# Expert value rows of two prompt tiles: one dense pass over the table in place of row gathers

## The chip, the core and the metric

One Trainium2 chip; the kernel runs on one of its cores. The metric is the device time of one execution in microseconds, the median of several. All data are fp32.

## What is computed

One layer of a decoder for 512 prompt tokens and 64 sample tokens (8 sequences of 8), D = 2048. The layer is: an input projection, latent attention (8 heads; the sample tokens also over 2048 cached tokens each) beside gated linear attention (4 heads), an output projection and residual; then the expert layer, and last an embedding gated by a sigmoid. What the change touches is the expert layer, cut from the reference:

```python
q = (xb @ w["peer_w_q"]).reshape(PEER_BLOCK, PEER_HEADS, 2, PEER_DKEY // 2)   # 8 heads
s1 = jnp.einsum("thd,kd->thk", q[:, :, 0], w["peer_keys1"])                    # 128 keys
s2 = jnp.einsum("thd,kd->thk", q[:, :, 1], w["peer_keys2"])                    # 128 keys
v1, i1 = lax.top_k(s1, PEER_TOPK)                                              # 16
v2, i2 = lax.top_k(s2, PEER_TOPK)
cand = (v1[..., :, None] + v2[..., None, :]).reshape(...)
cidx = (i1[..., :, None] * PEER_N_KEYS + i2[..., None, :]).reshape(...)
top_s, sel = lax.top_k(cand, PEER_TOPK)
e = jnp.take_along_axis(cidx, sel, -1)
gate = jax.nn.softmax(top_s.astype(F32), -1)
act = jax.nn.gelu(jnp.einsum("td,thkd->thk", xb, w["peer_u"][e]).astype(F32), approximate=False)
coef = (gate * act).astype(xb.dtype)
return jnp.einsum("thk,thkd->td", coef, w["peer_v"][e])
```

So every token picks 8 x 16 = 128 of 16384 experts, i.e. of 128 x 128 pairs of keys. It needs their rows of peer_u (for a dot product) and of peer_v (for a weighted sum). Each table has 16384 rows of 8 KB, 134.2 MB.

## The kernel before

Tokens lie in five tiles: 0 to 3 are prompt tiles of 128 tokens, 4 is the 64 sample tokens. They pass the mixer in groups, GROUPS = [[0], [1, 2], [3, 4]]. For a group, `mixer_loads` (SyncE), `mixing` (TensorE), `mixer` (VectorE and ScalarE) make the input projection, latent attention (for tile 4 the sample attention over cached pages), linear attention, the output projection and the query projection. This is the chain, all in the SBUF tile `front`. Weights come in slabs of 128 x 2048 (1 MB) into four buffers `W`, loaded by SyncE, each freed by the semaphore `slabs_used`. The input projection of group 1 is made ahead, beside the mixer of tile 0.

The queries give key scores. `best_keys` (VectorE) finds the best 16 of 128 keys for each head and side, `route` combines them to 16 experts a head with their gates and writes `idx_all` and `gate_all`, one column a pick.

The expert rows are gathered. A unit is one head of one prompt tile, 16 columns; the sample tile's 8 heads are folded into 4 units by spreading its 64 tokens on 128 partitions. For each column GpSimd issues an indirect DMA (`gathers`, L2540) that brings 128 rows of 8 KB, one for each token, into one of the RING = 8 buffers `ring`. VectorE takes it: a row of peer_u by one multiply-and-reduce with the token's input into `dots` (`dot_products`, L1968), a row of peer_v by a multiply-and-add into `total` (`weighted_sum`, L1993). Between the two, ScalarE applies GELU to the 16 dots of a unit and `gated` multiplies them with the gates. The order of gathers is GATHERS: unit u's peer_u rows, then unit u-1's peer_v rows. There are 36 units, so 576 gathers of each table.

VectorE and ScalarE must do the chain's steps and the gathers' work in one program order each. Tables of numbers set it: ROWS_BEFORE says, for each step of VectorE's chain, how many gathers are taken before it; STEPS_BEFORE says, for each unit, how many steps of ScalarE's chain come before its GELU; PAGES_BEFORE places the gathers of cached pages among GpSimd's. VectorE's order is walked so:

```python
def row_taken():
    rows_taken[0] += 1
    while steps_taken[0] < len(ROWS_BEFORE) and ROWS_BEFORE[steps_taken[0]] <= rows_taken[0]:
        step()
```

A step whose input is not there holds all that stands behind it, the gathers too; a gather's buffer is free only when VectorE has taken it.

At the end of a tile its sum is added to h in `xrow` and stored to `h2_dram` (`store_h2`, GpSimd). The gated embedding follows in groups, PLE_GROUPS = [[0, 1], [2, 3], [4]] (`embedding_loads`, `embedding`): h2 rows are loaded back, normed, projected with w_ple_gate (16 slabs) and w_ple_proj (2 slabs), and the result is stored. The last group, tile 4, has no store of h2 in between; its projection by w_ple_gate begins when the last gather is summed (`sample_embedding`).

## Time and profile before

| | us |
|---|---|
| median of 3 runs | 4337.45 |
| lowest and highest run | 4336.12, 4348.39 |
| span of the profiled execution (first to last instruction) | 4331.6 |
| VectorE (DVE) busy in the span | 3288.1 |
| TensorE (PE) busy | 2254.9 |
| GpSimd (POOL) busy | 2201.2 |
| ScalarE (ACT) busy | 522.0 |

The profiled execution has no run time of its own beside its span of 4331.6 us; the median lies 5.9 us above that span. The span is cut into windows by stage, in which the busy time of each engine, the granted clock of TensorE (1.00 is 2.4 GHz, 0.50 is 1.2 GHz) and what the 16 DMA engines moved can be read. A DMA share of 1.0 is all 16 engines busy all the time. The multiply-and-reduce of a gather leaves two records on DVE, one fp32 matmul leaves two on PE.

### The profile page before, as it was taken

The numbers are of one execution on the slowest core, as the hardware profiler recorded it, in microseconds if no ns is written. First come the engines' busy times: TensorE is split into PE (matmuls) and PEld (weight loads), VectorE is DVE, ScalarE is ACT, GpSimd is POOL, SyncE is SP. The second block draws the span as 40 slices with busy tenths as digits, with TensorE's granted clock in tenths as the row PEclk, the third lists the DMA queues.
The fourth block names the chain that finished last, engine by engine and source line by source line (L and its number), as shares of the span: only waits on it lengthen the run. The fifth ranks groups of instructions, "written<-read, shape, count | busy, mean of one in ns | idle before, by whom it ended". The sixth has DMA issues, their size and how long they took to land.

```text
span 4331.6 us, 24058 instructions
## 1 busy us (share of the span) xinstructions
PE 2254.9 (52%) x8238; PEld 1342.1 (31%) x8238; DVE 3288.1 (76%) x3700; ACT 522.0 (12%) x1098; POOL 2201.2 (51%) x1216
## 2 busy tenths in 40 slices
PE   8999815425899492779942457710000920000755
PEld 4456403213475131367731222710000410000322
DVE  0130699997667998868889856699999699988673
ACT  2220112122002001212212010000001000001001
POOL 0000365744332556468775653345667368877441
PEclk9999956657999796767865678955555965555877
DMA  8658789988997999989999899988989999999996
GB/s 294 250 223 287 303 357 364 422 323 335 424 423 299 422 424 414 353 356 365 406 374 360 347 400 413 405 345 339 399 365 405 424 415 422 422 407 422 424 408 234
DMA packets 261153, 1599.51 MB, mean 369 GB/s; under 512 B 27763, under 2 KB 49459, under 8 KB 91750
## 3 DMA queue, kind: packets, MB, share of 16 engines
q0 software_dynamic: 176064, 1268.30, 72.0%
q1 hardware_dynamic: 83078, 320.64, 19.5%
q10 hardware_dynamic: 1888, 9.03, 0.5%
q8 instruction: 65, 1.06, 0.1%
q14 instruction: 58, 0.48, 0.0%
HBM read 1554.75 MB, written 42.56 MB: 369 GB/s over the span
## 4 chain that ended last, share of the span: by engine, by line
PE 31%; DVE 30%; POOL 16%; DMA 13%; issue 7%; ACT 2%; SPq 0%; DVEq 0%; ACTq 0%; POOLq 0%
POOL ring L2549 16%; PE bank L826 14%; DVE ring L1968 11%; DVE total L1993 9%; DMA ring<-in_peer_v,idx_all 5%; DMA ring<-in_peer_u,idx_all 5%; PE bank L1251 4%; PE bank L1288 3%; PE bank L929 1%; PE bank L891 1%; PE bank L800 1%; PE bank L1079 1%; DMA front<-in_cache_kv_latent,page_rows 1%; DVE front L1744 1%; PE bank L1093 1%
## 5 line engine op out<-in xcount | busy, mean ns | idle before, releaser
L1993 DVE SCALAR_TENSOR_TENSOR total<-ring,gate_all,total 128x2048 f32<-128x2048 f32 x571 | 1341.8, 2350 | 188.0 <-DMA ring<-in_peer_v,idx_all 164.5
L2549 POOL DMA_INDIRECT ring<-in_peer_u,idx_all x576 | 1062.2, 1844 | 795.7 <-DVE total L1993 359.1
L2549 POOL DMA_INDIRECT ring<-in_peer_v,idx_all x576 | 1072.2, 1861 | 711.9 <-DVE total L1993 376.3
L1968 DVE CUSTOM_DVE_ANT_0 ring<-ring,xrow 128x2048 f32<-128x2048 f32 x576 | 1297.5, 2287 | 169.4 <-DMA ring<-in_peer_u,idx_all 167.5
L826 PE MATMUL bank<-front 128*128 128x512 f32 (+3 forms) x1920 | 838.3, 594 | 68.9 <-ACT front L2115 64.6
L800 PE MATMUL bank<-inv_diag,front 128*128 128x128 f32 (+1 forms) x304 | 61.9, 391 | 1159.3 <-DVE inv_diag L1378 1102.2
L826 PEld LDWEIGHTS bank<-front 128*128 128x128 f32 (+1 forms) x1920 | 338.4, 181 | 558.5 <-issue 554.5
L800 PEld LDWEIGHTS bank<-inv_diag,front 128*128 128x128 f32 (+1 forms) x304 | 58.9, 299 | 1164.2 <-DVE inv_diag L1378 1098.2
L1251 PE MATMUL bank<-front 128*128 128x128 f32 (+2 forms) x1536 | 257.0, 329 | 20.5 <-DMA front<-in_peer_w_q 17.4
L1251 PEld LDWEIGHTS bank<-front 128*128 128x128 f32 x1536 | 239.8, 192 | 39.3 <-DMA front<-in_peer_w_q 20.3
L2574 POOL DMA_DIRECT2D ring<-in_w_in x12 | 10.7, 894 | 342.8 <-PE bank L1288 239.6
L1373 DVE RECIPROCAL st<-st 128x1 f32<-128x1 f32 (+1 forms) x20 | 3.2, 161 | 225.8 <-ACT st L2049 225.8
L1288 PE MATMUL bank<-ring 128*128 128x490 f32 x384 | 163.8, 574 | 2.1 <-ACT front L2115 2.1
L2485 ACT ACTIVATE dots<-dots 128x16 f32<-128x16 f32 x36 | 7.7, 215 | 804.2 <-DVE dots L1968 759.3
L913 PE MATMUL bank<-ident,front 128*128 128x128 f32 (+1 forms) x20 | 4.6, 380 | 170.9 <-DVE front L1426 99.4
L1288 PEld LDWEIGHTS bank<-ring 128*128 128x128 f32 x384 | 70.4, 190 | 74.7 <-issue 71.6
L1196 PE MATMUL bank<-front 128*128 128x128 f32 (+1 forms) x288 | 41.7, 314 | 93.0 <-DVE front L1695 81.9
L2501 POOL DMA_DIRECT2D xrow<-xn_dram x6 | 3.4, 573 | 163.1 <-DMA z_dram<-total 102.7
L1079 PE MATMUL bank<-ident,front 128*128 128x128 f32 x256 | 74.8, 395 | 7.4 <-DMA front<-in_cache_kv_latent,page_rows 5.8
L1575 DVE MAX8 front<-front 128x8 f32<-128x128 f32 (+1 forms) x80 | 19.2, 281 | 76.4 <-ACT front L2325 75.5
L1415 DVE TENSOR_TENSOR g_mla<-g_mla 128x128 f32<-128x128 f32 x1 | 0.3, 291 | 100.3 <-DMA g_mla<-in_qk_gain_q 100.3
L1119 PE MATMUL bank<-front 128*64 128x256 f32 x256 | 70.5, 444 | 6.9 <-ACT front L2357 6.9
(323 smaller groups left out, 2894.0 us busy)
## 6 DMA issues: line engine op xcount, KB each, us to landing
front<-in_w_in SPq DMA_DIRECT2D x64, 980.0 KB, 8.4
front<-in_w_out SPq DMA_DIRECT2D x48, 1024.0 KB, 9.1
front<-in_peer_w_q SPq DMA_DIRECT2D x48, 1024.0 KB, 13.3
front<-in_w_ple_gate SPq DMA_DIRECT2D x48, 1024.0 KB, 9.1
ring<-in_w_in POOLq DMA_DIRECT2D x12, 1960.0 KB, 10.5
front<-in_w_uq SPq DMA_DIRECT2D x6, 1536.0 KB, 10.7
ring<-in_peer_u,idx_all POOLq DMA_INDIRECT x576, 14.3
ring<-in_peer_v,idx_all POOLq DMA_INDIRECT x576, 16.0
```

Of the source, the lines that this page charges most:

```text
L800: mm = e.matmul(out, row, inv_diag[:R, :R], start=True, stop=True)
L826: mm = e.matmul(bank[4 * sl + c][:R, 0:ncol], XT[:, k, sl * P:sl * P + R], W[:, n % SLABS, c * ncol:(c + 1) * ncol], start=(k == 0), stop= ...
L891: mm = e.matmul(bank[c][:R, :], XT[:, k, 0:R], W[:, n % SLABS, c * BANK:(c + 1) * BANK], start=(k == 0), stop=False)
L929: mm = e.matmul(bank[j][:R, 0:2 * QK], cqT[:, slot(t), k, 0:R], wq[:, k, j * 2 * QK:(j + 1) * 2 * QK], start=(k == 0), stop=(k == 3))
L1079: e.transpose(bank[k][:, j * P:(j + 1) * P], latb[:, i, k * P:(k + 1) * P], ident[:, :])
L1093: mm = e.matmul(S, lt[0:ROPE, 2, j * P:(j + 1) * P], qrT[0:ROPE, b, :], start=False, stop=True)
L1119: e.matmul(bank[7][0:NS, 0:KVR], pTs[:, pg, :], latb[:, pg % HALF, :], start=(pg == 0), stop=False)
L1251: mm = e.matmul(bank[j][:, 0:ntok], W[:, n % SLABS, at:at + P], XT[:, k, 0:ntok], start=(k == 0), stop=(k == KD - 1))
L1288: mm = e.matmul(bank[6 + sl][:, 0:IN_BANK], xt[:, k, sl * P:(sl + 1) * P], chunk(n)[:, k % 8, :], start=(k == 0), stop=(k == KD - 1))
L1968: e.tensor_tensor_reduce(out=ring[:, b, :], in0=ring[:, b, :], in1=xrow[:, t % 2, :], scale=1.0, scalar=0.0, op0=ALU.mult, op1=ALU.add, ac ...
L1993: e.scalar_tensor_tensor(out=total, in0=ring[:, b, :], scalar=c1, in1=total, op0=ALU.mult, op1=ALU.add).then_inc(s("summed"), 1)
L2549: e.indirect_dma_start(out=ring[:, k % RING, :], out_offset=None, in_=a[("peer_u", "peer_v")[side]][0], in_offset=bass.IndirectOffsetOnAxi ...
```

## The change

The peer_v rows of tiles 1 and 2 are no longer gathered. Their weighted sums are one matrix product: for each token a row of 16384 coefficients, zero but for its 128 picks, times the whole of peer_v, read once in 128 slabs of 128 rows. All peer_u rows, and the peer_v rows of tiles 0, 3 and 4, are gathered as before. The work stands behind the last group's routing, in this order:

1. `spread` for tile 1, later for tile 2: VectorE splits the picked expert number into its two key numbers (shift by 7, and with 127). TensorE transposes both and the coefficients, so that the 128 picks of a token lie on partitions. For each token VectorE makes two one-hot matrices 128 picks x 128 keys, the first scaled by the coefficient, and TensorE multiplies them: 128 x 128 coefficients of that token. Four tokens make a group, written to one PSUM bank; ScalarE copies it, and after each 16 tokens stores 1 MB to `c_dram`.
2. `expert_sums`: SyncE loads the 128 slabs of peer_v, and for every 8 slabs the coefficients of 256 tokens (`coefficients`, runs of 512 bytes); ScalarE turns them (`turned_coefficients`), and TensorE makes 8 matmuls of 128 x 512 a slab into all eight PSUM banks.
3. VectorE adds the banks to h of tiles 1 and 2, which are then the first embedding group: PLE_GROUPS = [[1, 2], [0, 3], [4]].

The gathers are now in tiles' order: both tables for tile 0, peer_u alone for tiles 1 and 2, both for tiles 3 and 4. The three tables of numbers are new. Some semaphores are merged, and the constant `iota16` (16 numbers) becomes `iota` (128).

```diff
+DENSE, SUMMED = [1, 2], [0, 3, 4]
+EB = 8
+GROUP = 4
+CHUNK = 16
+G_GROUPS = P // GROUP
+G_CHUNKS = P * len(DENSE) // CHUNK
...
 GATHERS = []
-for _u in range(UNITS):
-    GATHERS.append((_u, 0))
-    if _u:
-        GATHERS.append((_u - 1, 1))
-GATHERS.append((UNITS - 1, 1))
+for _t in range(T):
+    for _u in range(FIRST_UNITS[_t], FIRST_UNITS[_t + 1]):
+        GATHERS.append((_u, 0))
+        if _t in SUMMED and _u > FIRST_UNITS[_t]:
+            GATHERS.append((_u - 1, 1))
+    if _t in SUMMED:
+        GATHERS.append((FIRST_UNITS[_t + 1] - 1, 1))
...
@@ SyncE
+            def expert_rows(lo, hi):
+
+                for i in range(lo, hi):
+                    n = PASSES["dense"] + i
+                    e.wait_ge(s("slabs_used"), n - SLABS + 1)
+                    if n % SLABS in (PICKS_SLAB, ONEHOT_SLAB) and i < SLABS:
+                        e.wait_ge(s("g_psum"), G_GROUPS * len(DENSE))
+                    e.dma_start(W[:, n % SLABS, :], a["peer_v"][0][i * P:(i + 1) * P, :]).then_inc(s(f"w_landed{n % SLABS}"), 16)
+
+            def coefficients(b):
+
+                if b == 0:
+                    for i in range(2):
+                        e.wait_ge(s(f"c_stored{i}"), 16 * G_CHUNKS // 2)
+                if b >= 2:
+                    e.wait_ge(s("coefs_turned"), 2 * (b - 1))
+                e.dma_start(CB[b % 2].rearrange("p c i n -> p c (i n)"), c_dram[:, :, EB * b:EB * (b + 1), :].rearrange("c p i n -> p c (i n)"))\
+                    .then_inc(s(f"pair_landed{b % 2}"), 16)
...
@@ TensorE
+            def spread(j):
...
+                for q in range(G_GROUPS):
+                    n = j * G_GROUPS + q
+                    e.wait_ge(s("picks_spread"), n + j + 2)
+                    if n >= 2:
+                        e.wait_ge(s("g_staged"), n - 1)
+                    for i in range(GROUP):
+                        mm = e.matmul(bank[4 + n % 2][:, i * P:(i + 1) * P], onehot[:, n % 2, 1, i, :], onehot[:, n % 2, 0, i, :],
+                                      start=True, stop=True)
+                    mm.then_inc(s("g_psum"), 1)
+
+            def expert_sums():
+
+                e.wait_ge(s("g_staged"), G_GROUPS * len(DENSE))
+                for i in range(NKEY):
+                    n = PASSES["dense"] + i
+                    e.wait_ge(s(f"w_landed{n % SLABS}"), slab_landed(n))
+                    if i % (EB // 2) == 0:
+                        e.wait_ge(s("coefs_turned"), i // (EB // 2) + 1)
+                    for sl in range(len(DENSE)):
+                        cols = CT[:, i % EB, sl * P // CHUNK:(sl + 1) * P // CHUNK, :].rearrange("p c n -> p (c n)")
+                        for c in range(4):
+                            mm = e.matmul(bank[4 * sl + c][:, :], cols, W[:, n % SLABS, c * BANK:(c + 1) * BANK],
+                                          start=(i == 0), stop=(i == NKEY - 1))
+                    mm.then_inc(s("slabs_used"), 1)
...
@@ VectorE
+            def spread(j):
...
+                e.wait_ge(s("gates_ready"), j + 1)
+                if j == 0:
+                    e.wait_ge(s("slabs_used"), PASSES["dense"])
...
+                for q in range(G_GROUPS):
...
+                    for i in range(GROUP):
+                        k = GROUP * q + i
+                        e.tensor_scalar(onehot[:, n % 2, 0, i, :], iota[:, :], picksT[:, j, 0, k:k + 1], picksT[:, j, 2, k:k + 1],
+                                        ALU.is_equal, ALU.mult)
+                        ins = e.tensor_scalar(onehot[:, n % 2, 1, i, :], iota[:, :], picksT[:, j, 1, k:k + 1], None, ALU.is_equal)
+                    ins.then_inc(s("picks_spread"), 1)
...
                     dot_products(u, t)
-                    if u:
-                        weighted_sum(u - 1)
-            weighted_sum(UNITS - 1)
+                    if u > FIRST_UNITS[t]:
+                        if t in SUMMED:
+                            weighted_sum(u - 1)
+                        else:
+                            gated(u - 1)
...
@@ ScalarE
+            def turned_coefficients():
+
+                half = EB // 2
+                for m in range(NKEY // half):
+                    b, i = m // 2, m % 2 * half
+                    yield
+                    e.wait_ge(s(f"pair_landed{b % 2}"), 16 * (H_GLA // 2 + b // 2 + 1))
+                    if b:
+                        e.wait_ge(s("slabs_used"), PASSES["dense"] + EB * (b - 1) + i + half)
+                    e.copy(CT[:, i:i + half, :, :], CB[b % 2][:, :, i:i + half, :].rearrange("p c i n -> p i c n")).then_inc(s("coefs_turned"), 1)
```

How the instructions move is set by the tables of numbers. In the whole of VectorE's order the change has 576 gathers of peer_u and 320 of peer_v. At the chain's marks these many gathers have been taken, before and now: norm ahead of the output pass of tiles 1 and 2, 165 and 108; their routing, 240 and 180; mixer of tiles 3 and 4, 322 and 225; end of their latent attention, 381 and 262; end of the sample attention, 498 and 333; norm ahead of their output pass, 584 and 377; their routing, 664 and 435; first one-hot of tile 1, 436, of tile 2, 512 to 524; adds of the dense result, 725; last steps of the second embedding group, 1124 and 855.

VectorE, linear attention of tile 3, before (L1706 and L1707, L1694 and L1695 are steps of the chain; L1993 takes a gather, L1977 is `gated`):

```order
L1706 TENSOR_TENSOR front<-front 128x32x8
L1707 TENSOR_TENSOR front<-front 128x32x8
L1694 TENSOR_TENSOR front<-front 128x16x16
L1695 TENSOR_TENSOR front<-front 128x16x16
L1977 TENSOR_TENSOR gate_all<-dots,gate_all 128x16
L1993 SCALAR_TENSOR_TENSOR total<-ring,gate_all,total 128x2048
L1706 TENSOR_TENSOR front<-front 128x64x4
L1707 TENSOR_TENSOR front<-front 128x64x4
```

The same place in the change (these lines are now L1807, L1808, L1795, L1796):

```order
L1807 TENSOR_TENSOR front<-front 128x32x8
L1808 TENSOR_TENSOR front<-front 128x32x8
L1795 TENSOR_TENSOR front<-front 128x16x16
L1796 TENSOR_TENSOR front<-front 128x16x16
L1807 TENSOR_TENSOR front<-front 128x64x4
L1808 TENSOR_TENSOR front<-front 128x64x4
L1795 TENSOR_TENSOR front<-front 128x32x8
L1796 TENSOR_TENSOR front<-front 128x32x8
```

The gathers between the steps are gone; the whole block of level steps of this tile stands between two gathers.

VectorE, `best_keys` of tile 4, before (two key lists; L1993 takes gathers of peer_v):

```order
L1993 SCALAR_TENSOR_TENSOR total<-ring,gate_all,total 128x2048 x2
L1584 MAX front<-front 64x8 x2
L1587 MAX_INDEX front<-front 64x8 x2
L1589 CAST front<-front 64x32
L1993 SCALAR_TENSOR_TENSOR total<-ring,gate_all,total 128x2048
L1575 MAX front<-front 64x8 x2
L1993 SCALAR_TENSOR_TENSOR total<-ring,gate_all,total 128x2048
L1579 MAX_INDEX front<-front 64x8
L1580 MATCH_REPLACE front<-front 64x128
```

In the change, the end of `best_keys` of tile 4:

```order
L1685 MAX front<-front 64x8 x2
L1688 MAX_INDEX front<-front 64x8 x2
L1690 CAST front<-front 64x32
L1919 TENSOR_TENSOR front<-front 64x2048
L1924 MAX front<-front 64x8 x8
L1928 MAX_INDEX front<-front 64x8
L1929 MATCH_REPLACE front<-front 64x256
```

and, right behind the routing, the beginning of tile 1's one-hots (L2034 and L2036; L2104 takes a gather of peer_u):

```order
L1976 TENSOR_TENSOR gate_all<-front 64x64
L1978 TENSOR_TENSOR front<-front 64x64
L2022 TENSOR_SCALAR front<-idx_all 128x128
L2023 TENSOR_SCALAR front<-idx_all 128x128
L2024 CAST front<-front 128x256
L2104 ISA ring,dots<-ring,xrow 128x2048
L2104 ISA dots 128x1
L2034 TENSOR_SCALAR front<-iota,front 128x128
L2036 TENSOR_SCALAR front<-iota,front 128x128
L2034 TENSOR_SCALAR front<-iota,front 128x128
```

The routing of both tiles, spread over 161 gathers before, stands in one piece with no gather in it.

## Rows read from the trace of the kernel before

**Rows 1.** The page: busy shares, the 40 slices of DMA, bytes moved
```profile
PE 2254.9 (52%) x8238; PEld 1342.1 (31%) x8238; DVE 3288.1 (76%) x3700; ACT 522.0 (12%) x1098; POOL 2201.2 (51%) x1216
...
DMA  8658789988997999989999899988989999999996
GB/s 294 250 223 287 303 357 364 422 323 335 424 423 299 422 424 414 353 356 365 406 374 360 347 400 413 405 345 339 399 365 405 424 415 422 422 407 422 424 408 234
DMA packets 261153, 1599.51 MB, mean 369 GB/s; under 512 B 27763, under 2 KB 49459, under 8 KB 91750
```

**Rows 2.** Windows by stage: window, its length, busy us and records of each engine
```profile
core 0: us, PE busy (x) PEld busy (x) DVE busy (x) ACT busy (x) POOL busy (x), PEclk, DMA share, GB/s
0.00:578.00 578.00, 504.86 (x1839) 284.22 (x1839) 165.76 (x416) 102.94 (x236) 64.67 (x53) 0.96 0.74 269
578.00:1040.00 462.00, 163.37 (x594) 107.08 (x594) 432.11 (x465) 94.66 (x181) 287.29 (x146) 0.62 0.90 364
1040.00:1328.00 288.00, 254.36 (x928) 171.83 (x928) 185.48 (x151) 42.45 (x93) 89.24 (x67) 0.93 0.98 409
1328.00:1660.00 332.00, 238.85 (x576) 92.72 (x576) 297.64 (x557) 25.98 (x67) 159.30 (x93) 0.84 0.96 395
1660.00:1846.00 186.00, 92.61 (x284) 47.36 (x284) 172.01 (x186) 39.86 (x78) 114.05 (x58) 0.66 0.94 371
1846.00:2230.00 384.00, 334.11 (x1865) 271.34 (x1865) 314.20 (x257) 70.88 (x135) 290.34 (x143) 0.73 0.93 375
2230.00:2537.00 307.00, 76.40 (x302) 52.78 (x302) 257.93 (x299) 43.00 (x71) 186.85 (x90) 0.58 0.93 365
2537.00:2835.00 298.00, 236.52 (x928) 148.49 (x928) 198.30 (x145) 32.43 (x84) 123.17 (x82) 0.91 1.00 409
2835.00:3348.00 513.00, 0.00 (x0) 0.00 (x0) 506.44 (x715) 12.22 (x19) 303.02 (x177) 0.50 0.92 368
3348.00:3490.00 142.00, 132.40 (x340) 65.27 (x341) 94.02 (x64) 19.91 (x49) 54.21 (x41) 0.93 1.01 424
3490.00:3997.00 507.00, 7.05 (x17) 2.85 (x15) 459.56 (x314) 4.66 (x9) 416.18 (x198) 0.51 1.01 417
3997.00:4162.00 165.00, 137.44 (x356) 67.03 (x356) 116.70 (x88) 21.41 (x52) 72.35 (x49) 0.90 1.01 424
4162.00:4332.00 170.00, 76.89 (x210) 31.06 (x210) 87.94 (x56) 11.63 (x27) 40.47 (x25) 0.72 0.77 292
```

**Rows 3.** Groups of instructions by line: the two DVE passes of a gather
```profile
L1968 DVE CUSTOM_DVE_ANT_0 ring<-ring,xrow 128x2048 f32<-128x2048 f32 x576 | 1297.5, 2287 | 169.4 <-DMA ring<-in_peer_u,idx_all 167.5
L1993 DVE SCALAR_TENSOR_TENSOR total<-ring,gate_all,total 128x2048 f32<-128x2048 f32 x571 | 1341.8, 2350 | 188.0 <-DMA ring<-in_peer_v,idx_all 164.5
```

**Rows 4.** Timeline of ACT, chain, group of L826: second input pass of tiles 3, 4
```profile
1522.21 1.98 ACT L2115 COPY front<-bank 128x490 f32<-128x490 f32 x4 [96.75 <-DVE front L1589]
...
1522.92 113.10 PE bank L826 x256
...
L826 PE MATMUL bank<-front 128*128 128x512 f32 (+3 forms) x1920 | 838.3, 594 | 68.9 <-ACT front L2115 64.6
```

**Rows 5.** Groups by line and shape, and DVE's timeline: small instructions of DVE
```profile
L1575 DVE MAX8 front<-front 128x8 f32<-128x128 f32 x64 | 15.5, 283 | 76.2 <-ACT front L2325 75.5
L1378 DVE TENSOR_SCALAR inv_diag<-ident,st 128x128 f32<-128x128 f32 x12 | 3.6, 298 | 0.4
L1766 DVE COPY front<-front 128x8 f32<-128x8 f32 x32 | 2.9, 165 | 0.2
...
489.06 0.48 DVE L1575 MAX8 front<-front 128x8 f32<-128x128 f32 x2
```

**Rows 6.** Chain of waits: start us, us, what; the first gate pass
```profile
3370.47 111.84 PE bank L826 x256
```

**Rows 7.** DMA issues: size of one, us from issue to landing
```profile
front<-in_w_out SPq DMA_DIRECT2D x48, 1024.0 KB, 9.1
...
front<-in_state_gla SPq DMA_DIRECT2D x4, 1024.0 KB, 21.4
```

More of the change, by code:

```diff
@@ L107 @@
                    if g != AHEAD or k[:2] != "in"]
+                  + [("dense", NKEY)]
                   + [(f"gate{g}", KD + PLE // P) for g in range(len(PLE_GROUPS))]):
@@ L485, in pages_landed @@
         def pages_landed(u):
-            return 16 * sum(2 - v % 2 for v in range(u % PAGE_BUFS, u + 1, PAGE_BUFS))
+            ahead = 2 * AHEAD_RING // AHEAD_BUFS if u % PAGE_BUFS < AHEAD_BUFS else 0
+            return 16 * (ahead + sum(2 - v % 2 for v in range(u % PAGE_BUFS, u + 1, PAGE_BUFS)))
         def first_slot(u, side):
@@ L772, in _ @@
             e.wait_ge(s("sample_spread"), 32)
+            expert_rows(0, 2)
+            coefficients(0)
+            coefficients(1)
+            expert_rows(2, SLABS + 2)
+            for b in range(2, NKEY // EB + 1):
+                if b < NKEY // EB:
+                    coefficients(b)
+                expert_rows(EB * (b - 2) + SLABS + 2, EB * (b - 1) + SLABS + 2)
+            expert_rows(NKEY - EB + SLABS + 2, NKEY)
             for pg in range(len(PLE_GROUPS)):
@@ L853, in embed @@
                             mm.then_inc(s("embed_psum"), 1)
+            def spread(j):
+                e.wait_ge(s("picks_spread"), j * (G_GROUPS + 1) + 1)
+                for w in range(3):
+                    row = picks[:, j, w, :] if w < 2 else gate_all[:, row_units(DENSE[j])]
+                    mm = e.transpose(bank[7][:, w * P:(w + 1) * P], row, ident[:, :])
+                mm.then_inc(s("keysT_psum"), 1)
+                for q in range(G_GROUPS):
[20 more added lines that the diff above has]
+                    mm.then_inc(s("slabs_used"), 1)
+                e.wait_ge(s("v_added"), 4 * len(DENSE))
             def sample_embedding():
@@ L1331, in _ @@
                     now(mixing(g))
+            e.wait_ge(s("scores_sb"), 4 * T)
+            for j in range(len(DENSE)):
+                spread(j)
+            expert_sums()
             for pg, tiles in enumerate(PLE_GROUPS[:2]):
@@ L1887, in embedding @@
                     yield
+                if pg == 0:
+                    e.wait_ge(s("rows_loaded"), ROWS_IN["ffn", LAST] + 16 * len(DENSE))
+                    for sl in range(len(DENSE)):
+                        for c in range(4):
+                            cols = slice(c * BANK, (c + 1) * BANK)
+                            yield
+                            e.wait_ge(s("slabs_used"), PASSES["dense"] + NKEY)
+                            e.tensor_tensor(H[:, sl, cols], H[:, sl, cols], bank[4 * sl + c][:, :], ALU.add).then_inc(s("v_added"), 1)
+                    yield
                 yield from norm_rows("ple", tiles)
@@ L1925, in woven @@
                     yield from other_routes(g)
+                for j in range(len(DENSE)):
+                    yield from spread(j)
                 for pg in range(2):
@@ L2440, in woven @@
                     yield from other_routes(g)
+                for j in range(len(DENSE)):
+                    yield from spread(j)
+                yield from turned_coefficients()
                 for pg in range(2):
@@ L2476, in steps_to, with gelu, by_rows @@
                     passed[0] += 1
-            for u in range(UNITS):
+            def gelu(u):
                 t = TILE_OF[u]
-                hi = u - FIRST_UNITS[t] + 1
-                lo = hi - 1
-                steps_to(STEPS_BEFORE[u])
+                j = u - FIRST_UNITS[t]
+                yield
                 e.wait_ge(s("dots_done"), (u + 1) * TOPK)
-                d = dots[:, t % 2, lo * TOPK:hi * TOPK]
+                d = dots[:, t % 2, j * TOPK:(j + 1) * TOPK]
                 e.activation(d, d, ACT.Gelu).then_inc(s("gelu_ready"), 1)
+            def by_rows():
+                for t in range(T):
+                    for u in range(FIRST_UNITS[t], FIRST_UNITS[t + 1]):
+                        yield from gelu(u)
+            beside = by_rows()
+            next(beside)
+            for n in STEPS_BEFORE:
+                steps_to(n)
+                next(beside, None)
             for x in weave:
```

170 lines of the change are left out of this document (113 added, 57 removed), and 65 rows, old and new, of the table ROWS_BEFORE.

## The prediction

> **What bounds the kernel now.** The page comes first. DVE is busy 76% of the span, PE 52%, and the slices of DMA stand at 8 to 9 tenths nearly everywhere, with 422 to 424 GB/s where they are full [rows 1]. The kernel moves 1599.51 MB; at 424 GB/s that is 3772 us of a span of 4331.6, so the DMA engines are free for only 560 us. 1152 gathers of 128 rows of 8 KB (1.049 MB, 2.47 us at that rate) make 1208 MB of it. Each gather is taken by one pass on DVE, 2287 ns for a dot product, 2350 ns for a weighted sum [rows 3], 2.3 us on the mean, so on DVE a gather costs nearly what it costs in DMA.
>
> The windows by stage then say where which limit holds [rows 2]. I cut them at marks of the chain: mixer of tiles 1 and 2 (578 to 1040), its output pass and queries (to 1328), input pass of tiles 3 and 4 (to 1660), latent attention (to 1846), sample attention (to 2230), linear attention (to 2537), output pass and queries (to 2835). I call the end of the last queries Q, 2835 here. To Q the DMA moves 1019 MB (2404 us at 424), so it is free 431 us. From 2835 to 3348 PE does nothing and DVE is busy 506 of 513 us, at 368 GB/s; from there to 4162 DMA is full, 417 to 424 GB/s. The last 170 us run at 292 GB/s: 53 us free, the tail behind the last gather.
>
> So the time is bytes over 424 GB/s, plus the stretches in which DMA is free. I price both for the change.
>
> **The bytes.** 256 gathers of peer_v go (tiles 1 and 2): -268.4 MB. Their load of h and store of the sum go too: -4.2. The dense pass reads peer_v once, 128 slabs: +134.2. The coefficients, 16 pieces of 1.05 MB, go out and come back: +33.6. Total 1494.7 MB, 3525 us: 247 us less. DVE loses 256 x 2.35 = 602 us and gains 512 one-hot products.
>
> **The front, to Q.** Up to the last routing DVE's order in the change holds 435 gathers where it held 664; with those in the ring, 784 MB have then moved (1848 us). What matters is how far the chain shortens when the gathers between its steps go. Gathers per stage, counted in the two orders: 144 to 89, 75 to 72, 82 to 45, 59 to 37, 117 to 71, 86 to 44, 80 to 58. The floor of a stage is DVE's other work (its busy time less 2.3 us a gather) plus the gathers left, or PE's busy time if longer; the ceiling is its present length [rows 2].
> - 462 us: DVE 101 + 205 = 306. I take 350, DVE 87% busy (94% now), since the steps in between wait on PE and ACT.
> - 288 us: PE 254, DMA share 0.98, gathers unchanged: 288.
> - 332 us: PE's two passes of 113 us, with 64.6 us between them for ACT's copy, which itself waits 96.75 us for DVE's last key list [rows 4]. The routing now stands in one piece behind gather 185 and ends before the first pass does, so the 64 us go; 226 + 22 ahead + 25 for z to go out and back: 273.
> - 186 us: DVE 36 + 85 = 121; I take 145.
> - 384 us: PE is busy 334 us at a granted clock of 0.73; only the edges shrink: 362. Here the DMA is left idle most: 71 gathers in place of 117.
> - 307 us: DVE 60 + 101 = 161. The 42 gathers that go were 97 us, all on the path: 210.
> - 298 us: 409 GB/s now, so 122 MB less 23 MB is 233 us, PE 237; with the norms between the passes 260.
> With the 578 us ahead of them Q comes at 2466, 369 us earlier; floors alone give 2230, ceilings 2835. The DMA is then free 2466 - 1848 = 618 us of the front, 187 more than now.
>
> **From Q to the first dense matmul.** DVE goes alone through five pieces. The routing of tiles 3 and 4, now 16 heads with hardly a gather in between: DVE's 506 us of 2835 to 3348 less 174 gathers is 106 us, in which the ring of 8 fills and DMA stands. The one-hots of tile 1: 256 instructions. The nearest row is the same operation and shape, 298 ns alone (L1378); two MAX8 of 128 elements at 283 ns pass in about 0.5 us; an 8-element copy is 165 ns [rows 5]. I take 0.26 us: 67 us, and 11 gathers, 92 us (bounds 0.165 and 0.3: 42 to 77 us). Four tokens are eight of these, 2.1 us, and PE's four small matmuls and ACT's one copy for them should hide behind that; if they set the pace at 2.5 us a group, each tile costs 13 us more. Then 65 gathers at DMA rate, 161 us, with PE idle, because tile 2's gates need its last dot product. Its one-hots: 67 + 12 gathers, 95 us. The last store and the first load of coefficients: 15. Together 469 us: the dense pass starts at 2935. In 469 us 199 MB could move; only 113 are asked for (267 us), so DMA is free 202 us.
> The Trainium skill, page "VectorE: DVE Perf Modes", section on the fixed extra latency of instructions that read SBUF, gives 58 cycles plus 128 elements at two per cycle, 127 ns at 0.96 GHz: 65 us for all 512 in place of my 133. The row of L1378 is 298 ns, over twice that, and I stay with the rows.
>
> **The dense pass and the rest.** 1024 fp32 matmuls of 128x512 are 2048 records, as every fp32 matmul here leaves two; the gate pass runs 256 records in 111.84 us beside gathers [rows 6], its window at a granted clock of 0.93, so near the upper level of 2.4 GHz. So 895 us, 7.0 us a slab. Its slabs and pieces are 151 MB, which leaves room for 217 gathers in it; DVE's order puts the eight adds of its result behind gather 725, 201 after its start. Balanced within some 40 us, most of it covered by the ring: 10 us lost. DVE needs 201 x 2.3 = 462 us there, ACT's turning copies are covered. From the start of the pass 598 MB are left: 1410 us. A piece comes back in runs of 512 B; the loads and stores of 1 KB runs (in_state_gla, 21.4 us to landing against 9.1 for a slab of equal size [rows 7]) stand in the stage 2230 to 2537, where a DMA share of 0.93 moved only 365 GB/s: some 21 us lost on 8 MB, 2.7 us per MB. For 14 pieces 38 us; nothing if it hides, 14 x 12.3 = 172 if the whole difference in landing counts. The tail behind the last gather stays, 53. So 1410 + 10 + 38 + 53 = 1511, and the span ends at 4446. PE alone would be done earlier: 895, two gate groups of 142 us [rows 2] and the tail, so gathers still end the kernel.
> Against the profiled span of 4331.6 that is +114: bytes -247, front +187, behind Q 202 free in place of 68 (513 us at 368 GB/s), +134, piece loads +38, the turn +10, less the 8 us free now between 3490 and 3997. The median of the runs is 5.9 us over the span, so 4452 us.
> The Trainium skill has a rule against my rate too: its page "DMA: Bandwidth & Descriptors", section "Where 436 GB/s comes from", puts reads from HBM at about 358 GB/s for a core; by it the 598 MB would take 1670 us, 260 more. The trace shows 424 GB/s over whole slices, nearly all of it HBM reads, so the trace disagrees.
>
> **Rivals.**
> 1. Faster: the chain runs at its floors. For it: in every attention stage DVE is 82 to 94% busy [rows 2], so gathers, not latency, may be what it waits for. Against it: tables of steps that fix where DVE may take a gather leave it standing at each wait for PE or ACT. It decides where Q falls below 2338; at Q = 2240 the time is 4226, at 2338 it is 4324, 0.3% below the median. Chance 0.17.
> 2. No change (0.3%, 13 us, is about what a measurement of this kernel can tell from none): Q between 2338 and 2364. Chance 0.06.
> 3. Much slower: the coefficient loads cost their full 172 us, or ACT, which must take GELU and turning copies in a fixed order, holds PE and gathers in turns: 4452 + 134 = 4586 and more. A piece has to land within the 55 us of eight slabs. Chance 0.10.
> 4. The HBM limit above: 4712. Chance 0.03.
> The forecast, Q between 2364 and 2590, has 0.64.
>
> **Numbers.** Faster is rival 1, 0.17; same 0.06; slower 0.77. The range must leave out at most 2 in 10: from 4275 (Q at 2289, half of rival 1 kept) to 4590 (Q at 2604, or rival 3 begun).
>
> **What would show it.** In the new profile: 896 gathers and 1495 MB; Q near 2466 (last matmuls of the query keys); DMA well below 300 GB/s in the sample attention and between Q and the dense pass; one-hots at 0.26 us; 2048 records of the dense pass at 0.44 us, about 895 us from 2935; DMA full from there; gathers of tile 4 last. Wrong if Q is below 2338, if the dense pass takes over 1000 us, or if DMA is not full beside it.

## The result, and the profile after

| | median | runs |
|---|---|---|
| before | 4336.8 us | 4334.1 to 4348.4 |
| the change | 4706.3 us | 4700.7 to 4708.0 |

The ratio is 1.084, with a 95% interval of 1.083 to 1.086: 8.4% slower. The forecast was slower, 4452 us, at most 4590. So the direction was right and the size was not: 254 us are missing from the sum. The profiled execution has a span of 4704.8 us, against 4446 in the working, 259 us more. (The two differ by 5 us because the working put the median 5.9 us above the span, and it lies 1.5 us above.)

The page of the change, its slices of DMA and its DMA packets (before: [rows 1]):

```profile
PE   8999554388896689943972404459779798890746
DVE  0121877956786765587557999872552440369674
DMA  8766878599869886578991498998988975599996
GB/s 292 250 233 243 323 305 334 216 422 419 350 233 419 315 331 257 212 280 324 416 387 73 170 404 357 377 415 312 409 311 316 381 289 208 215 405 422 421 410 254
DMA packets 277493, 1495.03 MB, mean 318 GB/s; under 512 B 26035, under 2 KB 80627, under 8 KB 122918
```

The bytes are as worked out. The mean rate is not: slices 28 to 35 of the 40 fall as low as 208 GB/s, and they lie in the dense pass, where DMA should be full.

The windows by stage (bounds and length, busy time of PE, PEld, DVE, ACT and POOL, granted clock, DMA share, GB/s), for the stages of [rows 2]; the last three are from Q to the dense pass, the dense pass, and the rest:

```profile
578.00:960.00 382.00, 171.91 (x629) 114.49 (x630) 317.34 (x379) 97.37 (x197) 176.41 (x94) 0.63 0.77 295
960.00:1259.00 299.00, 259.19 (x960) 177.36 (x959) 188.49 (x186) 44.70 (x107) 92.78 (x74) 0.92 1.02 417
1259.00:1545.00 286.00, 226.06 (x525) 81.06 (x526) 212.25 (x483) 17.91 (x44) 70.92 (x45) 0.89 0.78 305
1545.00:1680.00 135.00, 93.73 (x293) 47.16 (x293) 120.27 (x132) 32.96 (x63) 66.00 (x38) 0.73 0.82 315
1680.00:2024.00 344.00, 328.18 (x1846) 268.68 (x1846) 197.13 (x217) 72.97 (x134) 141.54 (x89) 0.76 0.70 268
2024.00:2245.00 221.00, 84.43 (x351) 59.75 (x351) 169.70 (x261) 49.59 (x104) 117.16 (x52) 0.62 0.83 311
2245.00:2500.00 255.00, 222.36 (x828) 135.94 (x829) 128.75 (x118) 20.40 (x46) 77.12 (x56) 0.93 0.95 387
2500.00:2992.00 492.00, 117.47 (x572) 104.99 (x570) 474.72 (x1193) 77.64 (x87) 190.69 (x107) 0.57 0.65 257
2992.00:4078.00 1086.00, 901.93 (x2048) 396.40 (x2048) 426.16 (x278) 33.18 (x38) 267.49 (x185) 0.91 0.83 324
4078.00:4705.00 627.00, 353.84 (x923) 165.52 (x922) 433.20 (x312) 59.02 (x136) 281.88 (x169) 0.78 0.94 376
```

The front is close: the seven stages were put at 350, 288, 273, 145, 362, 210 and 260 us, together 1888, and take 1922. Q is 2500 in place of 2466. From Q to the dense pass are 492 us in place of 469. The dense pass takes 1086 us in place of 895, though PE is busy as forecast, 902 us. Behind it are 627 us, where the working had 616 (4446 less 2935 and 895). So the 259 us are 34 + 23 + 191 + 11, and the dense pass is three quarters of it.

The groups and waits of the dense pass (line, engine, operation, busy us, mean ns, idle before and its causes; then who waited for what: us, times, longest):

```profile
L947 PE MATMUL bank<-front 128*128 128x512 f32 x2048 | 902.3, 604 | 222.7 <-DMA front<-in_peer_v 183.7 <-ACT front L2562 38.9
L2562 ACT COPY front<-front 128x1024 f32<-128x1024 f32 x32 | 33.3, 1045 | 1029.4 <-PE bank L947 999.4 <-DMA front<-c_dram 30.0
...
DVE gate_all L2114 <- ACT dots L2667: 327.6, 4, 105.4
```

PE stands for slabs of peer_v 8 times, 184 us. DVE stands 328 us for GELUs, and behind this window, at the adds of the dense result (L1996), 204 us more for PE. Two causes offer themselves. **Theory A:** the slabs come late because a piece of coefficients, in runs of 512 B, stands ahead of them in SP's queue, and DVE's waits follow from that. **Rival B:** ACT's fixed order of GELU and turning copies holds DVE and PE in turns; the prediction had it in its rival 3.

SP's queue (L798 loads a piece, L789 a slab), ACT's turning copies and PE around one piece (start, length, count, idle before):

```profile
3271.54 0.43 SPq L798 DMA_DIRECT2D front<-c_dram  x1
3278.04 48.40 SPq L789 DMA_DIRECT2D front<-in_peer_v  x8
3326.47 0.44 SPq L798 DMA_DIRECT2D front<-c_dram  x1
3332.97 19.82 SPq L789 DMA_DIRECT2D front<-in_peer_v  x1
```

```profile
3339.90 1.04 ACT L2562 COPY front<-front 128x1024 f32<-128x1024 f32 x1 [26.42 <-PE bank L947]
3397.41 1.04 ACT L2562 COPY front<-front 128x1024 f32<-128x1024 f32 x1 [56.47 <-PE bank L947]
```

```profile
3380.84 19.48 PE L947 MATMUL bank<-front 128*128 128x512 f32 x39 [27.30 <-DMA front<-in_peer_v]
```

The piece of 3271.54 was in after 8.0 us. At that time the gathers stood still, because DVE waited for a GELU. The GELU came at 3285.9, the gathers ran again, and the piece of 3326.47 took 49.4 us. From the issue of a piece PE has four slabs, 4 x 6.87 = 27.5 us. The fifth is issued behind the piece, at 3332.97, and is in at 3380.8, 4.9 us after it: PE stands 27.3 us. With 8.0 us there is nothing to wait for, as at 3271.54.

A wait costs PE a little more than its length. The two stretches of 7 us behind this one:

```profile
3381.00:3388.00 7.00, 7.00 (x11) 2.98 (x12) 0.00 (x0) 0.00 (x0) 0.00 (x0) 0.65 1.01 422
3388.00:3395.00 7.00, 7.00 (x17) 3.04 (x16) 0.00 (x0) 0.00 (x0) 0.00 (x0) 1.00 1.01 420
```

After 27.3 us without a matmul the granted clock is 0.65 on the mean, between its two levels of 1.2 and 2.4 GHz, and 11 records fit in where 17 do at 1.00. Six records of 0.43 us are 2.6 us, and 27.3 + 2.6 is the 30 us by which the turning copy's idle time, 56.47, exceeds 26.42. Behind the other seven waits the granted clock of the first 7 us is 0.60 to 0.77.

The eight waits are 27.0, 28.7, 27.1, 3.9, 27.3, 27.4, 27.3 and 15.0 us. The 16 pieces took 8.0 to 9.4 us six times, 23.0 to 39.2 four times and 49.2 to 49.4 four times; the second and third, close behind others, took 71.7 and 74.7.

### The profile page after: what moved, and what is told of

Read it like the earlier page. It is cut to its first block, busy times and chain, and to the rows that moved or that the text cites. A ratio compares the mean times of both kernels' runs of the same rounds, so it can differ in the third digit from the quotient of the medians.

```text
span 4704.8 us, 29317 instructions
## 1 busy us (share of the span) xinstructions
PE 3264.5 (69%) x10804; PEld 1836.0 (39%) x10804; DVE 2829.9 (60%) x3968; ACT 608.7 (13%) x1185; POOL 1544.1 (33%) x956
## 2 busy tenths in 40 slices
DMA packets 277493, 1495.03 MB, mean 318 GB/s; under 512 B 26035, under 2 KB 80627, under 8 KB 122918
## 4 chain that ended last, share of the span: by engine, by line
PE 57%; DMA 16%; DVE 15%; POOL 5%; issue 3%; ACT 2%; SPq 1%; another core or an unknown queue 1%; DVEq 0%; ACTq 0%; POOLq 0%
PE bank L890 18%; PE bank L947 16%; DMA front<-in_peer_v 6%; POOL ring L2743 5%; PE bank L1348 4%; PE bank L1385 4%; DVE ring L2104 4%; DVE total L2134 2%; DMA front<-in_peer_w_q 1%; DMA ring<-in_peer_v,idx_all 1%; PE bank L1216 1%; DVE front L2034 1%; PE bank L864 1%; PE bank L1176 1%; PE bank L1190 1%
## 5 line engine op out<-in xcount | busy, mean ns | idle before, releaser
L2104 DVE CUSTOM_DVE_ANT_0 ring<-ring,xrow 128x2048 f32<-128x2048 f32 x576 | 1302.6, 2287 | 284.3 <-DMA ring<-in_peer_u,idx_all 282.8
L2743 POOL DMA_INDIRECT ring<-in_peer_u,idx_all x576 | 957.5, 1662 | 1552.4 <-DVE dots L2104 1196.2
L947 PE MATMUL bank<-front 128*128 128x512 f32 x2048 | 902.3, 604 | 222.7 <-DMA front<-in_peer_v 183.7
L2743 POOL DMA_INDIRECT ring<-in_peer_v,idx_all x320 | 530.9, 1659 | 1022.6 <-DVE total L2134 606.6
L2134 DVE SCALAR_TENSOR_TENSOR total<-ring,gate_all,total 128x2048 f32<-128x2048 f32 x317 | 745.2, 2351 | 188.6 <-DMA ring<-in_peer_v,idx_all 178.9
L947 PEld LDWEIGHTS bank<-front 128*128 128x128 f32 x2048 | 396.4, 194 | 728.0 <-issue 537.6
L1348 PEld LDWEIGHTS bank<-front 128*128 128x128 f32 x1536 | 242.3, 193 | 34.2 <-DMA front<-in_peer_w_q 16.7
L924 PE MATMUL bank<-ident,front 128*128 128x128 f32 x4 | 1.3, 441 | 271.9 <-DVE front L2024 271.9
L2562 ACT COPY front<-front 128x1024 f32<-128x1024 f32 x32 | 33.3, 1045 | 1029.4 <-PE bank L947 999.4
L932 PE MATMUL bank<-front 128*128 128x128 f32 x512 | 109.6, 392 | 64.0 <-DVE front L2036 64.0
L932 PEld LDWEIGHTS bank<-front 128*128 128x128 f32 x512 | 98.3, 286 | 75.7 <-DVE front L2036 75.1
L1996 DVE TENSOR_TENSOR front<-front,bank 128x512 f32<-128x512 f32 x8 | 4.9, 679 | 203.6 <-PE bank L947 203.6
```

The lines of the kernel that those rows point to most:

```text
L932: mm = e.matmul(bank[4 + n % 2][:, i * P:(i + 1) * P], onehot[:, n % 2, 1, i, :], onehot[:, n % 2, 0, i, :], start=True, stop=True)
L947: mm = e.matmul(bank[4 * sl + c][:, :], cols, W[:, n % SLABS, c * BANK:(c + 1) * BANK], start=(i == 0), stop=(i == NKEY - 1))
L1348: mm = e.matmul(bank[j][:, 0:ntok], W[:, n % SLABS, at:at + P], XT[:, k, 0:ntok], start=(k == 0), stop=(k == KD - 1))
L2104: e.tensor_tensor_reduce(out=ring[:, b, :], in0=ring[:, b, :], in1=xrow[:, t % 2, :], scale=1.0, scalar=0.0, op0=ALU.mult, op1=ALU.add, ac ...
L2134: e.scalar_tensor_tensor(out=total, in0=ring[:, b, :], scalar=c1, in1=total, op0=ALU.mult, op1=ALU.add).then_inc(s("summed"), 1)
L2743: e.indirect_dma_start(out=ring[:, k % RING, :], out_offset=None, in_=a[("peer_u", "peer_v")[side]][0], in_offset=bass.IndirectOffsetOnAxi ...
```

## The experiments

All runs are set against runs of the kernel before on the same chip. Start and end of the dense pass are those of its matmuls in each trace.

| run | median us | ratio to before | pass from, to | length | pass end to span end |
|---|---|---|---|---|---|
| the change | 4706 | 1.084 | 2992, 4078 | 1086 | 626 |
| contiguous layout | 4478 | 1.033 [1.031, 1.035] | 2966, 3848 | 882 | 628 |
| pieces from ACT's queue | 4553 | 1.048 [1.046, 1.050] | 2999, 3928 | 929 | 628 |
| adds at 750 | 4721 | 1.088 [1.086, 1.090] | 2991, 4091 | 1100 | 625 |
| GELUs earlier | 4721 | 1.088 [1.086, 1.089] | 2982, 4092 | 1110 | 626 |
| contiguous, adds at 742 | 4480 | 1.033 [1.031, 1.036] | 2965, 3847 | 882 | 628 |
| 50 gathers ahead | 4420 | 1.019 [1.017, 1.021] | 2899, 3779 | 881 | 630 |
| 77 gathers ahead | 4404 | 1.014 [1.011, 1.017] | 2892, 3774 | 882 | 628 |
| 50 ahead, adds at 742 | 4420 | 1.019 [1.017, 1.021] | 2910, 3793 | 882 | 624 |
| 77 fitted into waits | 4351 | 1.003 [1.002, 1.004] | 2842, 3724 | 882 | 627 |
| the same, whole tail moved | 4319 | 0.996 [0.994, 0.997] | 2847, 3728 | 881 | 597 |
| the same, 512-B layout | 4559 | 1.051 [1.049, 1.052] | 2856, 3955 | 1099 | 597 |
| two pieces only | 4537 | 1.046 [1.044, 1.048] | 2980, 3890 | 911 | 628 |

### What holds the dense pass

**Contiguous layout.** The scratch tensor is laid out by piece:

```diff
-c_dram = scratch("c_dram", G_CHUNKS, P, NKEY, CHUNK)
+c_dram = scratch("c_dram", NKEY // EB, P, G_CHUNKS, EB * CHUNK)
-e.dma_start(c_dram[c], stage[c % 2])
+e.dma_start(c_dram[:, :, c, :].rearrange("b p m -> p b m"), stage[c % 2].rearrange("p (b i) n -> p b (i n)", i=EB))
-... c_dram[:, :, EB * b:EB * (b + 1), :].rearrange("c p i n -> p c (i n)")
+... c_dram[b].rearrange("p c m -> p (c m)")
```

> The coefficients lie in DRAM by piece: each chunk is stored in runs of 512 B, each piece comes back in one run of 8 KB per partition. Bytes and order are unchanged. Theory A (a piece in runs of 512 B stands in SP's queue ahead of the slabs of peer_v, and PE runs out of its four slabs): the eight waits of some 30 us go, the dense pass takes 895 to 930 us in place of 1086, and the kernel 4706 - 180 = 4525 us. Rival B (ACT's fixed order of GELU and turning copies is what costs): the pass gets shorter, but the gathers still wait for GELUs and the total gains less than 60 us, 4650 or more. Rival C (the 512 B runs cost wherever they are): the stores take 25 us each in place of 4, the start of the pass moves by over 60 us.

The time fell by 229 us, 49 more than expected, and the pass, 882 us, is 13 us below its range. The windows of the dense pass and of the rest:

```profile
2992.00:3600.00 608.00, 608.00 (x1418) 269.19 (x1417) 334.32 (x218) 23.56 (x26) 135.25 (x144) 1.00 1.01 421
3600.00:3848.00 248.00, 248.00 (x579) 109.63 (x577) 97.78 (x64) 8.59 (x10) 40.67 (x42) 1.00 0.92 379
3848.00:4476.00 628.00, 355.56 (x923) 166.08 (x922) 433.39 (x312) 59.02 (x136) 280.12 (x169) 0.78 0.93 376
```

PE never stops, and DMA stands at 421 GB/s beside it: what the prediction described. DVE waits for no GELU any more, with the order of ACT unchanged. The first piece moved too; in the chain of the change and of this run:

```profile
2954.50 3.86 DMA c_dram<-front
2958.42 32.70 DMA front<-c_dram
```

```profile
2950.46 5.08 DMA c_dram<-front
2955.61 9.59 DMA front<-c_dram
```

The runs of 512 B are now in the stores, with few gathers in flight. They cost 1.2 us on the chain, and the median landing time of the 16 stores is 5.9 us in place of 4.2; rival C falls with B. The number of packets is the same in both traces, 277493, and a load of 512-B runs with no gather in flight took 8.0 us, so it is not the small runs as such, nor that they are loads, but small runs in competition.

**Pieces from ACT's queue,** in the old layout:

```diff
-for b in range(2, NKEY // EB + 1):
-    if b < NKEY // EB:
-        coefficients(b)
-    expert_rows(EB * (b - 2) + SLABS + 2, EB * (b - 1) + SLABS + 2)
-expert_rows(NKEY - EB + SLABS + 2, NKEY)
+expert_rows(SLABS + 2, NKEY)
...
 e.copy(CT[:, i:i + half, :, :], ...).then_inc(s("coefs_turned"), 1)
+if i and b + 2 < NKEY // EB:
+    e.wait_ge(s("coefs_turned"), 2 * (b + 1))
+    e.dma_start(CB[b % 2]..., c_dram[:, :, EB * (b + 2):EB * (b + 3), :]...)
```

> The layout is left as it is (runs of 512 B come back), but pieces 2 to 15 are issued by ACT behind its own turning copies, in ACT's queue, so no slab stands behind one in SP's queue. Theory A: like the contiguous layout, pass 895 to 930 us, total near 4525. If instead the runs of 512 B slow everything that is in flight with them, the waits stay: slabs and gathers land late whatever the queue, pass 1030 us or more, total over 4650.

153 us less; the pass, 929 us, is in its range, the total 28 us above 4525. PE's waits for slabs went. One of 30 us is left, at the first pieces, which SP still issues. So the order in SP's queue was the cause. But now slabs run beside the piece as well as gathers: while gathers run, seven pieces in a row land 61 to 63 us apart, and one piece lasts PE 54.9 us. Each is issued before its predecessor is in and stands behind it in ACT's queue, so the time from issue to landing climbs from 56 to 116 us, and ACT waits for pieces in its turn:

```profile
ACT front L2558 <- DMA front<-c_dram: 391.7, 9, 60.9
```

Most of that is covered by the two buffers. PE's starts behind a wait:

```profile
2998.47 16.37 PE L943 MATMUL bank<-front 128*128 128x512 f32 x32 [37.31 <-ACT front L2558]
3044.98 483.96 PE L943 MATMUL bank<-front 128*128 128x512 f32 x1120 [30.13 <-DMA front<-in_peer_v]
3529.23 55.17 PE L943 MATMUL bank<-front 128*128 128x512 f32 x128 [0.29 <-ACT front L2558]
3592.23 112.59 PE L943 MATMUL bank<-front 128*128 128x512 f32 x256 [7.83 <-ACT front L2558]
3707.54 219.97 PE L943 MATMUL bank<-front 128*128 128x512 f32 x512 [2.73 <-ACT front L2558]
```

The first lies ahead of the pass. Inside it ACT's waits cost PE 11 us. The pass is 47 us longer than in the contiguous layout: 30 + 11, and 6 us more of matmuls (888 against 882). Both halves of theory A show here: the place in the queue, and a landing time that depends on the company.

**Adds at 750, and GELUs earlier.** Each edits one table of the change:

```diff
-... 526, 727, 727, ... 727, 728, 728, 731, 731, 765, ...
+... 526, 750, 750, ... 750, 751, 751, 754, 754, 765, ...
```

```diff
-... 398, 401, 407, 412, 417, 423, 428, 442, ...
+... 398, 401, 405, 409, 413, 417, 421, 442, ...
```

> The eight adds of the dense result stand behind gather 750 in DVE's order in place of 727; nothing else moves. DVE was idle 204 us in front of them with its ring full. Theory A: 23 more gathers are taken in that idle time, so 23 x 2.47 = 57 us less, 4649 (bounds 4640 and 4680). Rival (the end is set by the gate groups of PE behind the pass, not by gathers): no gain, 4706 within 10.

> ACT's order has four turning copies between the GELUs of tile 3 in place of five and six; the adds stay behind gather 727. Theory A: DVE's waits for GELU (328 us) shrink by two thirds, but DVE then stands at the adds for as much longer, because the pass still ends at 4078: total 4706 within 15. Rival B (the GELU order is the cause of the loss): 4706 - 150 = 4556 or less. If PE is held by GELUs instead, the pass gets longer than 1086 us and the total over 4725.

Neither gained; both are some 15 us slower than the change, with PE's eight waits for slabs at 197 and 208 us in place of 184. Theory A's number for the adds, 57 us, was wrong, and the time is 5 us above the rival's range too. For the GELUs 4706 within 15 held; their waits inside the pass fell from 328 to 164 us, by half and not by two thirds. The pass grew to 1110 us, but PE's waits in it are for slabs, not for GELUs. In the first DVE's wait moved from the adds to the GELUs, in the second from the GELUs to the adds; the rows of the one, then of the other:

```profile
DVE gate_all L2115 <- ACT dots L2668: 414.5, 6, 105.0
```

```profile
DVE front L1996 <- PE bank L947: 368.6, 1, 368.6
```

DVE is tied to PE at two places, and both hang on the same slow pass. Rival B is refuted: with ACT's order loosened the kernel is no faster, and with that order kept and the layout changed it is 229 us faster.

**Two pieces only.**

```diff
-                if b < NKEY // EB:
-                    coefficients(b)
...
-                    ... 16 * (H_GLA // 2 + b // 2 + 1))
+                    ... 16 * (H_GLA // 2 + 1))
```

This kernel leaves out most of the sums of tiles 1 and 2.

> The change with pieces 2 to 15 of the coefficients not loaded: every turning copy reads one of the first two pieces, so the sums of tiles 1 and 2 are left out of the computation in all but their first 16 slabs; the matmuls, copies and slabs are all there. Layout and order are the change's. Theory A: no piece stands ahead of a slab, the pass takes 883 to 900 us, and 14.7 MB less are 35 us: 4478 - 35 = 4443 within 20. Rival (PE waits for slabs because gathers crowd them): pass 1000 us or more, over 4600.

The pass takes 911 us, 11 over its range and far below the rival's 1000: one wait, 27.4 us, is left at the first pieces. The total was 94 us above the expected one, and 60 above the contiguous layout, though 14.7 MB less are moved. In the two profiled executions the difference is 42 us, all of it at the end of the pass (3890 and 3848): DVE reached the adds early and stood there 184 us, against 76 in the contiguous layout. So bytes taken off the DMA here bring nothing: the end of the pass decides.

The last column of the table says the same. In every run but the two with all of DVE's fixed places behind the pass moved, the span ends 624 to 630 us after the pass, whatever happened before, and also where the adds alone were moved.

### The stretch ahead of the pass

The contiguous layout is still 137 us slower than the kernel before. PE never stops in its pass, so what remains is looked for ahead of the pass and in the tail.

**50 and 77 gathers ahead of Q.** The places of the sample attention in DVE's table are stretched evenly, gathers 262 to 333 over 121 places or 148; page loads and GELUs are shifted with them.

> The contiguous layout, with 50 of the 77 gathers that stood between Q and the dense pass put into the sample attention (their places stretched from 71 to 121 gathers), the page loads and GELUs shifted with them. Theory A (the DMA engines are free there because DVE's order leaves the gathers out, and PE is the limit): the stage stays near 344 us, Q near 2505, the dense pass starts 50 x 2.47 = 123 us earlier, total 4478 - 123 = 4355. Rival (the chain there is bound by the latency of its small steps, and each gather on DVE delays it): Q comes 50 x 2.3 = 115 us later and the total stays at 4478.

> The same with all 77 gathers. The sample attention would then hold 148 gathers, 340 us of DVE and 34 us of other work, more than its 344 us. Theory A: the last 27 cost the chain what they save behind Q, so 4355 within 25. Rival: 4478 or more.

The gains are 58 and 73 us; both runs lie between theory A and rival (4420 for 4355 or 4478, 4404 for 4355 within 25 or 4478 and more). The windows of the sample attention (with a little of the next stage) in the contiguous layout, with 50 and with 77:

```profile
1680.00:2059.00 379.00, 336.26 (x1871) 273.54 (x1869) 215.19 (x237) 82.09 (x147) 159.27 (x100) 0.74 0.72 275
```

```profile
1678.00:2112.00 434.00, 340.43 (x1871) 276.13 (x1869) 324.44 (x341) 85.19 (x152) 272.97 (x150) 0.70 0.90 358
```

```profile
1685.00:2171.00 486.00, 354.72 (x1869) 288.38 (x1868) 383.79 (x395) 90.63 (x158) 332.07 (x177) 0.66 0.94 380
```

DMA fills up, but the stage grows from 379 to 434 to 486 us: the routing behind Q came 53 and 105 us later, 1.1 us for each of the first 50 gathers and 1.9 for each of the next 27.

**Fitted into waits.** From 578 us to Q the waits of DVE for PE, ACT or a store add up to 294 us in the trace of the contiguous layout; in the sample attention they are mostly 2.5, 4.4, 4.8 and 6.2 us long. This run puts the 77 gathers in front of such steps.

> The contiguous layout with all 77 gathers of tile 2 ahead of Q again, but each put in front of a step of DVE that waited at least 1 us for PE, ACT or a store in the trace of the contiguous layout (48 in the sample attention, 29 at nine longer waits of the other stages), and none elsewhere. Theory A (an added gather costs the chain nothing only where DVE stood for over 2.3 us; stretching the places evenly put half of them where it did not): Q at most 30 us later, the dense pass 150 to 180 us earlier, total 4478 - 165 = 4313. Rival (every gather on DVE or in the DMA delays the chain by 1 us or more wherever it stands, as 50 gathers cost 53 us): Q 77 us or more later, total 4375 or more.

The pass starts 124 us earlier, not 150 to 180, and the kernel takes 4351 us; the routing still came 52 us later. So 0.7 us for each gather: better placed than evenly, not free. Half of it is in the sample attention, whose window is 405 us long with 48 gathers more and 379 without. The theory was right in direction and 38 us too cheap. Why a gather placed in a wait still costs that much was not taken apart: DVE's pass and the gather's share of the DMA are both possible.

**The tail.** First the adds alone, then every fixed place behind the pass (adds 727 to 742, the steps at 765 to 785, 820 to 830, 855 to 865):

> The contiguous layout, with the eight adds of the dense result behind gather 742 in place of 727. In the contiguous layout alone DVE still stood 76 us at the adds. Theory A (with full DMA beside the pass a wait of DVE costs what the gathers would have moved): 15 gathers in 76 us, 15 x 2.47 = 37 us less than 4478, 4441. Rival (what stands behind the pass, two gate groups of PE, sets the end): 4478 within 10.

> Both edits, 50 gathers into the sample attention and the adds behind gather 742. If the two losses are separate stretches of free DMA, they add: 4478 - 37 - 123 = 4318 us, just under the kernel before (4337). If one takes the place of the other, 4355.

> The same, and every fixed place behind the dense pass moved, not the first alone: adds behind gather 742, the two gate groups' steps 10 to 20 gathers later. With the adds alone moved, DVE's 76 us at the adds came back as 66 us at the first gate group, and nothing was gained. Theory A: some 20 to 35 us less than the run without this edit. Rival (PE's chain of gate groups sets the end): no gain.

The adds alone brought nothing, with 50 gathers ahead (4420 us again, not 4318 or 4355) or without. DVE's wait for them fell from 76 to 16 us and came back at the next fixed place, the products of the first gate group:

```profile
DVE front L2013 <- PE bank L913: 65.8, 2, 65.3
...
DVE front L1997 <- PE bank L948: 16.4, 1, 16.4
```

With all places moved the second wait falls to 12 us, pass end to span end is 597 us in place of 627, and the kernel takes 4319 us, 32 less than without this edit, as expected. That is 0.4% faster than the kernel before (ratio 0.996, interval 0.994 to 0.997). The windows around the end of the pass without this edit and with it:

```profile
3600.00:3724.00 124.00, 123.95 (x289) 54.53 (x287) 29.51 (x18) 3.25 (x4) 13.09 (x13) 1.00 0.83 335
```

```profile
3600.00:3728.00 128.00, 128.00 (x299) 56.43 (x297) 67.46 (x46) 3.25 (x4) 28.76 (x29) 1.00 1.01 421
```

**The 512-B layout again,** in this best order.

> The fastest order so far (77 gathers fitted into waits ahead of Q, fixed places behind the pass moved), with the layout of the coefficients as the change has it, in runs of 512 B. Theory A (a piece that lands beside gathers takes 49 us, three slabs of 6.87 us are in SBUF by then, so PE stands 49 - 21 = 28 us; where DVE stands for a GELU the piece takes 8 us and PE does not wait): again some eight waits of 28 us, the pass 1060 to 1110 us in place of 883, total 4319 + 200 = 4520 within 30. Rival (the loss belonged to the old order of gathers, which this run has given up): under 4420.

4559 us, 240 more than the same order with the contiguous layout, and 9 beyond the range expected. The pass is 1099 us long, with the same eight waits:

```profile
PE bank L948 <- DMA front<-in_peer_v: 197.3, 8, 28.3
```

So the layout costs 229 us in the one order of gathers and 240 in the other, two orders that end 159 us apart in the contiguous layout: the loss did not belong to the change's order.

## Why the prediction was wrong in size

- **The bytes** were right to 0.3 MB.
- **The front** was 34 us too short (Q 2500, forecast 2466). The first mixer was 32 us too cheap (382, not 350), and the rest balanced out within 18 us each. The forecast that the sample attention would leave the DMA most idle held: 268 GB/s.
- **From Q to the dense pass,** 492 us for 469. The 65 gathers took 152 us for 161, and the one-hots 0.23 us each (two start every 0.46 us) for 0.26. The routing burst was 15 us longer, and the first coefficient load took 33 us beside gathers, where 15 stood for store and load together. The rest was not taken apart.
- **The dense pass** is the step that failed; its sign, "if the dense pass takes over 1000 us", came. PE's own time was close, 902 us for 895, and the pass runs in 882 when nothing holds it. What failed is the term for the coefficient loads, "For 14 pieces 38 us", with an upper bound of 172. It priced a piece by what its small runs cost in DMA time. In truth the pieces cost 204 us of pass (1086 less 882) by what stands behind them in SP's queue: 184 us in which PE waits for slabs, and 20 us more of matmuls, made at a lower granted clock right after the waits. The prediction had even put a number to a deadline, in its rival 3: "A piece has to land within the 55 us of eight slabs." That is the time until the piece itself is needed. The slab behind it is needed after 27.5 us, and it lands after the piece: a piece that took 23.0 us caused no wait, one of 28.5 us a wait of 3.9, those of 49 us waits of 27. The nearest row that the prediction had, 21.4 us for small runs [rows 7], lies just inside that deadline; what it did not show is what the gathers of this pass do to such a load.
- **Rival 3** named both halves, coefficient loads and ACT's order, at a chance of 0.10. The first half was it, but with more than the 172 us that it allowed, and for another reason than the one given. The second, as the two runs on tables show, only decided where DVE stood idle.
- **Rival 4** has a sum, 4712 us, that lies 6 us from the measured median. That is luck. Its mechanism, a lower limit for reads, is not there: in the contiguous layout DMA moves 421 GB/s for 608 us of the pass, and 1435 of all 1495 MB are reads.
- **The tail** was 616 us in the working and 627 in the trace. But its reason, "gathers still end the kernel", was wrong in this order. The fixed places behind the pass tied it to the end of the pass, and moving them gave 30 us. (The adds stand behind gather 727 in the table, not 725.)
- **The sum in the contiguous layout** is 4478 us, 26 over the forecast. But there the 38 us for small runs have no place, and without them the working gives 4414. So the rest of it was 64 us too short, 1.4%: the pass starts 31 us later than forecast, and from its start to the end of the span are 1510 us where the working without the pieces has 1473.

## What to carry to other kernels

Price a transfer not only by its bytes, but by its landing time in the company it will have, and ask of the transfer behind it in the same queue when that one is needed. If a piece of data is stored once and read back under load, put the small runs on the side where the DMA engines have nothing else to do. In an order written out by hand a removed wait comes back at the next fixed place, so move all places behind it together, and read from the trace where an engine stood before you add work to it.

## What was not expected of the hardware

- **A load of small runs loses its share to large ones.** The same 1 MB in 2048 runs of 512 B landed in 8.0 us with no gather in flight and in 49.4 us beside gathers of 8 KB rows; beside gathers and slabs seven such loads landed 61 to 63 us apart. Spread over 16 engines it is 128 runs each: 49.4 / 128 = 0.386 us a run, against 0.063 us alone. The difference, 0.32 us, is about the time that one engine needs for one row of 8 KB at 421/16 = 26.3 GB/s, 0.31 us. As an estimate, each small run waited for one large one. The Trainium skill, page "DMA: Bandwidth & Descriptors", section "Queues, rings and completion order", says that a DMA engine takes turns between the queues it has work for and changes only after a whole packet. The 49.4 us agree with that if a packet holds one run, and so the profile counts them: in the contiguous layout SP's queue has 30720 packets fewer, which is 16 x (2048 - 128).
- **Another issuing engine helped without more bandwidth.** Moving the pieces from SP to ACT gave 153 us. The same page, under "Rules for kernel authors", says that spreading DMAs over the issuing engines does not help bandwidth. The trace does not contradict that: what was gained is the order of landing.
- **A gather is not free on an engine that waits.** With 77 gathers in front of steps that stood for PE, ACT or a store (2.5 to 6 us in the sample attention), each still cost the chain 0.7 us on the mean, though DVE's pass of 2.3 us is shorter than these waits.
